# Moving the generation of the state-space matrices from the mixer into the FFN ahead of it, on GpSimd

## The reference, cut to what matters

```
for l in range(2):                                    # two layers, 512 latent and 256 context tokens, width 1024
    x, xc = x + 0.5 * gate * rms(swiglu(pre(x))), ...         # FFN 1 (1024 -> 2 x 2816 -> 1024)
    h = pre(x) @ w_in[l]                              # 512 SSM channels and 512 Fourier channels
    lam_bar = exp(lam * dt);  b_bar = ((lam_bar - 1) / lam) * b      # weights alone
    y_ssm = glu(d_skip * u + sum over both directions of Re(C @ scan(lam_bar, b_bar @ u)))
    y_f   = real(fft2(h_fourier)) @ w_fmix[l]
    x = x + gate * rms(concat(y_ssm, y_f) @ w_out[l])
    x = x + 0.5 * gate * rms(swiglu(pre(x)))                  # FFN 2
```

## Time and profile before

| | |
|---|---|
| median of 3 runs | 3126.36 us (3124.43 to 3127.66) |
| the profiled execution | 3122.22 us, with a span of 3120.4 us |
| mean granted TensorE clock | 0.924 of 2.4 GHz |
| TensorE matmul busy | 2833.4 us (91%) |
| VectorE busy | 1733.7 us (56%) |
| ScalarE busy | 696.0 us (22%) |
| GpSimd busy | 390.3 us (13%) |
| DMA | 313.84 MB, mean 101 GB/s |

### The profile page before, as it was taken

The page is one execution under the profiler, slowest core; times in us unless marked ns, Lnnn a source line. Parts: engine busy times, 40 slices in busy tenths (PEclk is TensorE's granted clock), DMA queues, the critical chain, the costliest instruction groups (busy, mean ns, idle before and its releaser), DMA issues.

```text
span 3120.4 us, 41582 instructions
## 1 busy us (share of the span) xinstructions
PE 2833.4 (91%) x16334; PEld 2627.6 (84%) x16334; DVE 1733.7 (56%) x2513; ACT 696.0 (22%) x921; POOL 390.3 (13%) x609
## 2 busy tenths in 40 slices
PE   6999999977987879999999799999977877899997
PEld 4999999966856869999999799999966656688886
DVE  5766666576354386666665633333367545544444
ACT  4211111132202231111112311111133102322222
POOL 1000000027702100000001000000027622100001
PEclk9999999986796989999999899999987686899998
DMA  7443333213353224343431122221222463223331
GB/s 254 135 126 117 121 121 121 81 34 125 126 187 95 61 68 126 111 127 114 128 114 56 39 64 64 60 67 54 70 44 95 149 194 84 66 88 94 101 94 47
DMA packets 343593, 313.84 MB, mean 101 GB/s; under 512 B 52544, under 2 KB 318664, under 8 KB 338888
## 3 DMA queue, kind: packets, MB, share of 16 engines
q1 hardware_dynamic: 280136, 204.59, 22.1%
q10 hardware_dynamic: 59264, 89.07, 8.7%
q0 software_dynamic: 4096, 18.88, 1.7%
HBM read 280.58 MB, written 31.92 MB: 100 GB/s over the span
## 4 chain that ended last, share of the span: by engine, by line
PE 78%; DVE 9%; POOL 6%; DMA 2%; ACT 2%; issue 2%; SPq 0%; ACTq 0%; DVEq 0%; POOLq 0%
PE ps L434 69%; PE ps L1131 2%; PE ps L560 2%; PE ps L807 1%; PE ps L1177 1%; DVE tmpN L885 1%; DMA E_d<-EG 1%; DVE rmsX L894 1%; DVE xT L773 1%; DVE hL L903 1%; DVE tmpN L911 1%; ACT wH L419 1%; POOL raw L1078 1%; DVE zb L1530 1%; DVE zd L1531 1%
## 5 line engine op out<-in xcount | busy, mean ns | idle before, releaser
L434 PE MATMUL ps<-hH,wH 128*128 128x384 f32 (+1 forms) x2880 | 1004.1, 349 | 66.9 <-DVE hL L903 46.3
L434 PE MATMUL ps<-hL,wH 128*128 128x384 f32 (+1 forms) x2880 | 997.3, 346 | 0.0
L434 PE MATMUL ps<-hH,wL 128*128 128x384 f32 (+1 forms) x2880 | 996.5, 346 | 0.0
L426 DVE TENSOR_TENSOR wL<-raw,wH 128x1024 fp32r<-128x1024 f32 x300 | 366.5, 1234 | 522.2 <-ACT wH L419 520.8
L434 PEld LDWEIGHTS ps<-hH,wH 128*128 128x128 f32 x2880 | 549.1, 191 | 90.6 <-issue 49.4
L434 PEld LDWEIGHTS ps<-hL,wH 128*128 128x128 f32 x2880 | 549.1, 191 | 18.0
L434 PEld LDWEIGHTS ps<-hH,wL 128*128 128x128 f32 x2880 | 548.2, 190 | 18.2
L419 ACT ACTIVATE wH<-raw 128x1024 fp32r<-128x1024 f32 x300 | 310.7, 1050 | 580.5 <-PE ps L434 576.4
L434 PE MATMUL ps<-midH,wH 128*128 128x384 f32 (+1 forms) x1232 | 423.8, 344 | 9.8 <-DVE wL L426 9.8
L434 PE MATMUL ps<-midH,wL 128*128 128x384 f32 (+1 forms) x1232 | 423.2, 343 | 0.0
L434 PE MATMUL ps<-midL,wH 128*128 128x384 f32 (+1 forms) x1232 | 423.1, 343 | 0.0
(11 more groups left out here) (252 smaller groups left out, 2436.9 us busy)
## 6 DMA issues: line engine op xcount, KB each, us to landing
raw<-in_ffn_gu_dram SPq DMA_DIRECT2D x176, 512.0 KB, 3.9
adaW<-in_w_ada_dram ACTq DMA_DIRECT2D x40, 1536.0 KB, 7.0
raw<-in_ffn_down_dram SPq DMA_DIRECT2D x88, 512.0 KB, 3.7
raw<-in_w_in_dram SPq DMA_DIRECT2D x16, 512.0 KB, 4.3
VT_d<-VTm ACTq DMA_DIRECT2D x8, 1024.0 KB, 3.9
W_d<-W ACTq DMA_DIRECT2D x8, 1024.0 KB, 5.0
raw<-in_w_out_dram SPq DMA_DIRECT2D x16, 512.0 KB, 4.4
VTs<-VT_d SPq DMA_DIRECT2D x8, 1024.0 KB, 5.4
```

Source lines behind the costliest of these rows:

```text
L426: nc.vector.tensor_tensor(wL[:, n % SPLIT_SLOTS, :], raw[:, n % RAW_SLOTS, :], wH[:, n % SPLIT_SLOTS, :].bitcast(f32), ALU.subtract).then_ ...
L434: ins = nc.tensor.matmul(dst, a, b, start=first and n == 0, stop=last and n == 3 * len(pairs) - 1)
```

## The change

1. The whole generation leaves the mixer. It becomes `gen_*` and runs in F1_0 (for M0) and F1_1 (for M1), cut into 8 pieces (quarter and direction) of half the size. V, W, b_bar, the pivots and the phases are made by GpSimd (`gen_pool`); TensorE's transposes of a piece stand inside a step's down product after m=3, its lags behind the down product; ScalarE copies out of PSUM.
2. Room: the tables take the place of `xT` in SBUF during the FFN. GpSimd stores `xT` to scratch `x_d` first (3 MB), and loads it back after the last piece; the norm after the FFN waits for it. PSUM's banks 6 and 7 go to the generation, so these two FFNs have three slots in place of four. `raw` has three slots everywhere.
3. The lags now use stationary tiles of 64 x 32 (`Bw`, half zeros) that go to four column groups of the array in turn, where they were 64 x 16 tiles in one column group.
4. D is added to the strip's centre by GpSimd (`skip_lag`), so `skip` and its reload of u are gone.
5. The loops over FFN steps are unrolled. SyncE's order in the mixer is new: the tables of quarter 0 are loaded before the projections end.
6. The small loads: `crow` takes 2 DMAs for a layer, not 32, and TensorE reorders it with 32 products against the identity.

```diff
-RAW_SLOTS, SPLIT_SLOTS = 4, 3
+RAW_SLOTS, SPLIT_SLOTS = 3, 3
+PIECES = 2 * HC
...
+        F.gen = Section("gen", GEN_COUNTS) if gen else None
+        F.slots = 3 if gen else 4
...
     def ffn_tensor(pe, F, pre):
...
+        for s in range(NPH - 1):
+            for i in range(4):
+                ride = F.ride0 + 2 * s + i // 2 if F.ride0 is not None and i % 2 == 0 else None
+                gate_up(4 + 6 * s + i, 4 + 12 * s + i, ride)
+            piece = s - 1 if F.gen and 1 <= s <= PIECES else None
+            down(8 + 6 * s, 8 + 12 * s, s, None if piece is None else lambda: gen_turn(pe, F.gen, piece))
+            if F.gen and s == 0:
+                gen_columns(pe, F.gen)
+            if piece is not None:
+                gen_lags(pe, F.gen, piece)
...
+        def lag_term(c0, c1, a, dd, rhs, first, last):
+            for p in range(QP):
+                for g2 in range(2):
+                    half = slice(g2 * NST, (g2 + 1) * NST)
+                    ins = nc.tensor.matmul(ps[32 * p:32 * p + 32, 6 + g2, c0:c1], Bw[half, a, dd, p, :], rhs(half, a, dd, p),
+                                           start=first, stop=last)
...
+    def gen_pool(pool, F):
...
+        pool.wait_ge(h_lo, KC * F.pre.nth + KC)
+        pool.dma_start(x_d, xT[:].rearrange("p k t -> p (k t)")).then_inc(x_spill, 16)
+        pool.wait_ge(x_spill, S.n0["x_spill"] + 16)
...
+        def state_in(i):
...
+            if i:
+                pool.wait_ge(vt_ps, S.n0["vt_ps"] + i)
+                pool.wait_ge(vt_store, S.n0["vt_store"] + 16 * i)
...
+        for i in range(PIECES):
+            state_in(i)
+            if i and i % 2 == 0:
+                skip_lag(i // 2 - 1)
+            state_out(i)
+            if i == 0:
+                pivots()
+            phases(i)
+        skip_lag(HC - 1)
...
+        pool.dma_start(xT[:].rearrange("p k t -> p (k t)"), x_d).then_inc(x_back, 16)
...
     def mix_tensor(pe, M, pre):
...
-        for q in range(HC):
-            if q:
-                proj(2 * q)
-                proj(2 * q + 1)
-            matrices(q)
-
+        for m in range(2, 8):
+            proj(m)
...
         for q in range(1, HC):
             turn(q)
-            if q >= 2:
-                skip(q - 2)
             turn_back(q, 0, zb, zd, ALU.subtract, True)
-        skip(HC - 2)
```

More of the change, by code:

```diff
@@ L325, in __init__, with make_ffn @@
             made[kind] += 1
-    def make_ffn(tag, layer, gu, down, tok0, ride0):
+    def make_ffn(tag, layer, gu, down, tok0, ride0, gen):
         nonlocal unit
@@ new lines, in tile_slot, with wait_tile @@
+    def tile_slot(F, g):
+        return g % F.slots
+    def wait_tile(pe, F, g):
+        if g < 4:
+            pair, part = 0, g
+        elif (g - 4) % 12 < 4 and g < 4 + 12 * (NPH - 1):
+            pair, part = (g - 4) // 12 + 1, (g - 4) % 12
+        else:
+            done = 12 * (NPH - 1) if g >= 4 + 12 * (NPH - 1) else 12 * ((g - 4) // 12) + 4
+            p, m = min((g - 4) // 12, NPH - 1), g - 4 - done
+            pe.wait_ge(down_read, F.n0["down_read"] + KC * (p + 1) + m + 1)
+            return
+        if part % 2 == 0:
+            pe.wait_ge(gate_read, F.n0["gate_read"] + 2 * pair + part // 2 + 1)
+        else:
+            pe.wait_ge(up_read, F.n0["up_read"] + 2 * pair + part // 2 + 1)
@@ new lines, in ffn_tensor, with gate_up, down @@
+    def ffn_tensor(pe, F, pre):
+        def gate_up(i, g, ride):
+            if g >= F.slots:
+                wait_tile(pe, F, g - F.slots)
+            if ride is not None:
+                ada_columns(pe, ride, 2 * tile_slot(F, g), TOK // 2)
+            n = F.base + i
+            pe.wait_ge(w_lo, n + 1)
+            wh, wl = wtile(n)
+            project(F.tok0, tile_slot(F, g), [(wh[:, k, :], wl[:, k, :]) for k in range(KC)], hH, hL).then_inc(w_used, 1)
+        def down(i, g, p, between=None):
+            n = F.base + i
+            pe.wait_ge(w_lo, n + 2)
+            pe.wait_ge(mid_lo, F.n0["mid_lo"] + 2 * p + 2)
@@ L664, in ffn_scalar @@
         for j in range(2):
[L665 to L676 removed]
+            gate(2 * j, 2 * j, j, None)
@@ new lines, in ffn_scalar @@
+            up(2 * j + 1, j)
+        for s in range(NPH - 1):
+            for j in range(2):
+                i, f = 4 + 6 * s + 2 * j, 2 + 2 * s + j
+                gate(i, 4 + 12 * s + 2 * j, f, None if F.ride0 is None else F.ride0 + 2 * s + j)
+                up(i + 1, f)
+            piece = s - 1 if F.gen and 1 <= s <= PIECES else None
+            if piece is not None:
+                gen_take_turned(act, F.layer, F.gen, piece)
+            split_hi(act, F.base + 8 + 6 * s + 3)
+            split_hi(act, F.base + 9 + 6 * s + 3)
+            if F.gen and s == 0:
+                gen_take_columns(act, F.gen)
+            if piece is not None:
+                gen_take_lags(act, F.gen, piece)
@@ L733, in ffn_vector @@
-        loop(dve, F, body, 0 if F.ride0 is None else 1)
-        down(4 + 12 * BODIES, 0, NPH - 1)
+            up(2 * j + 1, 2 * j + 1, j)
+        for s in range(NPH - 1):
+            more = F.ride0 is not None and s < NPH - 2
+            if F.ride0 is not None:
+                ada_steps(dve, F.ride0 + 2 * s + 1, 0, STEPS)
+            for j in range(2):
+                i, g, f = 4 + 6 * s + 2 * j, 4 + 12 * s + 2 * j, 2 + 2 * s + j
+                if j and more:
+                    ada_steps(dve, F.ride0 + 2 * s + 2, 0, KC)
+                split_lo(dve, F.base + i + 3)
+                up(i + 1, g + 1, f)
+            down(8 + 6 * s, 8 + 12 * s, s, F.ride0 + 2 * s + 2 if more else None)
@@ L1004, in mix_sync @@
         sp.wait_ge(y_ps, M.n0["y_ps"] + HC)
-        for i in range(12, 18):
-            load_unit(sp, i, 0, M.base, units[i])
+        load_units(12, 18)
     STATE_SEGS = ((0, 0, NCH - 1, slice(1, NCH)), (1, 0, CCH - 1, slice(CCH - 2, None, -1)),
@@ L1585, in rest_g @@
             tt(gL[:, m, 0:T], G[:, m, 0:T], gH[:, m, 0:T].bitcast(f32), ALU.subtract).then_inc(g_lo, 1)
-        for m in range(HC - 1):
+        for m in range(HC):
             rest_g(m)
-        skip(HC - 1)
-        rest_g(HC - 1)
         def times_gate(m):
```

703 lines of the change are left out of this document (331 added, 372 removed).

## The result

| | median of 4 runs | range |
|---|---|---|
| before | 3126.98 us | 3124.43 to 3127.66 |
| after | 2991.86 us | 2989.59 to 2992.80 |

The ratio is 0.9568, with a 95% interval from 0.9552 to 0.9585: 135 us faster, where 87 had been forecast. One execution of a later variant (e1_spill_early) took 6359.7 us for a reason that no trace shows, and no reading uses it. The profiled execution of the changed kernel has a span of 2987.4 us, 133.0 less than before.

The account below looks back on a forecast made before the run. TensorE was taken to bound F1_0 and F1_1, while engines waited on each other in the mixers' generation. 3122 - 201 of gains + 114 of costs = 3035 us, 3039 as median; range 2980 to 3115 us.

Parts of the forecast that it names:

- rival 2: Both FFNs: additions are cheap, tiles overlap by more than two, GpSimd hardly holds VectorE; 59 us added, 2984 us; chance 0.19.
- Mixers: M0 and M1: the generation's stretch shrinks to the projections left, gaining 93.5 us and 103.7 us.
- `skip`: Both mixers: removing these VectorE instructions gains 4 us, with nothing to 6 possible.
- TensorE's added work: F1_0 and F1_1: transposes 7.2, columns 2, lags 16, waits and shape changes 5, together 30 us in each FFN.
- overlap by two: Lags in F1_0 and F1_1: tiles overlap by about two, as L1194's do, so 2.0 us a piece, 16 for eight.
- overlap by eight: Lags in F1_0 and F1_1: if tiles ran eight at a time, TensorE's additions would be 20 us in each FFN.
- GpSimd against VectorE: F1_0: GpSimd's instructions hold VectorE's ada steps and splits, so TensorE waits: 41 us, from nothing to 87; F1_1 2 us.
- Three slots: F1_0 and F1_1: one PSUM slot fewer makes a down product's fourth tile wait, 5 us and 1 us.
- The spill: Start of F1_0: storing xT (3 MB) alongside the first two ada loads costs 5 us, between 0 and 12.
- Reload and raw slots: The reload of xT hides behind the FFN's last step, and three raw slots cost nothing.
- rival 4: F1_0 and F1_1: the clock falls behind each piece, 57 us for each FFN, 3153 us; chance 0.09.
- Rival 3: F1_0: VectorE becomes the bound, 69 us a step against TensorE's 57, costing 96 us; 3089 us; chance 0.16.

Follow-up runs that it names:

- e1_spill_early: The changed kernel, but GpSimd starts the spill of xT when the first chunk of the FFN's input is ready, not the eighth: median 2982.2 us.
- e4: The changed kernel, but lags go through all terms of one 64 x 32 tile before the next tile: median 3025.1 us.
- e2: The changed kernel, but in F1_0 GpSimd's 12 products and sums of each piece work on 64 of 512 columns: median 2971.5 us, F1_0 16.4 shorter.
- e3: The changed kernel, but each of GpSimd's 8 products of a piece is made twice, in both FFNs: median 3027.5 us, F1_0 37.5 longer.

## Why the prediction was right, and where not

The sign was right, and so were the gain in the mixers and the kinds of cost that the sum names. The range (2980 to 3115) held the time, but only as it reached down to rival 2: the number lay 47 us too high, outside the forecast's own 3005 to 3070 and 8 us from rival 2's 2984. Two terms were mis-sized, the overlap of the lags and what a hold costs.

- **Mixers**, 93.5 and 103.7 us: 92.7 and 101.3. The Fourier weights stood 51.4 and 41.0 us behind projection 1 (51 and 39 forecast); M1 lost 2 us in two waits for ScalarE, 0.58 and 0.69 us, and the slower products behind them. There was no wait for UC, VTs or the DFT.
- **`skip`**, 4 us: the two mixers' later parts are 9.9 us shorter. 5.5 of it stand between the Fourier weights and the states, which now run nearer to the full level (a gain that the forecast had cancelled against SyncE's loads); 4.4 are left for `skip`.
- **TensorE's added work**, 30 us for each FFN: 17.9 in F1_1, that is 2.0 for the columns (2.02 in the chain) and 2.0 a piece for transposes (0.87), lags and changes of shape. The step that failed is the overlap by two, taken from L1194. The lags took 0.55 and 1.13 us in turn, 0.8 in the mean where 2.0 was taken; that is 9 of the 12 us. The serial price was right as far as a run shows it (e4's slow pieces took 4.49 us where 4.6 was reckoned), and the wide ones overlap by 32 x 0.095 / 0.4 = 8 (the first to the last start, 0.4 us). Of the Trainium skill's rules in "TensorEngine Tiling (Array Packing)", Key Properties, that of the independent tiles gave 4 us a layer, an estimate. About 7 were measured, as the short ones overlap less (64 records in 0.6 us, serially 1.6). The waits and changes of shape, put at 5 us, took under 2. A slip besides: with overlap by eight the sum gives 18 us and not 20.
- **GpSimd against VectorE**, 41 us: e2 gives 16 for the wide instructions. The mechanism holds: ada rows alternate, splits are held, L720 is not. The step that failed is the number of holds times their price. I counted ten ada rows in a ride and added a whole instruction of GpSimd, 1.3 us, for each. In the four steps with a wait seven rows were held, at 0.9 us each, and the two splits lost 1.3 us together: 12.5 + 7 x 0.9 + 1.3 = 20.1 us, where I had 26. Measured from the end of the down product, TensorE could start the columns after 19.5 to 20.4 us. It came at 18.9 us (20.2 forecast, since the lags are shorter), so it waited 0.6 to 1.5 us and not 6. In the steps between, six rows were held and it did not wait. In step 0 twelve were held and it waited 6.1 us (8 forecast). The mean of 1.0 us for the ada rows was 0.81. The Trainium skill, "SBUF — State Buffer", Who interferes with whom, says that whichever of the two engines starts first keeps the shared port pair for its whole instruction. The trace agrees on which rows are held, but not in full on the price: one after the other a free ada row and a free product would take 0.54 + 1.18 = 1.72 us from start to start, and 1.44 were measured. It also says that a row with one input contends if it runs in a mode that takes two ports, and `tensor_scalar` can. The trace agrees in that L522, with one input, went from 0.42 us to 1.44 beside a product; the mode itself is in no row.
- **Three slots**, 5 and 1 us: 2.7 us of waits and none. **The spill**, 5 us: 8 us of wait, worth 6.1 in F1_0 when taken away. The 3 MB of the spill and the 3 MB of ada loads went together, which puts VectorE's first row off from 88.61 to 98.98 us. **Reload and raw slots**, 0: the norm behind F1_0 took 37.0 us as before, and F2_0's 3.3 us more are for the most part two stretches at a lower clock (96 products in 18.34 and 18.50 us, 16.77 and 16.96 before).
- **The clock.** What rival 4 expected did not come: F1_1 ran at 1.00 from 1790 to 2255 us, through all eight pieces. But behind VectorE's waits F1_0 lost some 11 us, a term that the sum did not have.
- **Rivals.** Rival 2 described both failed steps (59 us in the FFNs; 68 measured). Against it I had set that GpSimd starts just as the ada steps do. That is true, and e3 shows what it costs once the slack is gone. Rival 3's bound was not reached: VectorE was busy for 465 of 643 us.

Together: 81 - 50 = 31 us in F1_0, 33 - 18 = 15 in F1_1 and 3 in the mixers make 49 of gain that the forecast lacked. The other FFNs and the norms took 3 of it back.

## What to carry to other kernels

When two engines lock each other out, read the price of a hold from a stretch in which they alternate: the distance from one row's start to the next, less the same distance where the row is free. Here it was 0.9 us, and the other engine's instruction is 1.1 us long. Then count how many rows are held ahead of a deadline, since only these matter. Compute how late that stretch may end, and put the other engine's long instructions elsewhere: here the same instructions in another order were worth 8 us in F1_0. Behind each short wait look for a stretch at the lower clock, which can cost as much as the wait. Move a large spill to where the DMA engines are idle, not to where the next loads start.

## What was not expected of the hardware

- Lags on eight tiles of 64 x 32: 16 instructions of 112 columns start within 0.4 us whether they go round the tiles or through them one by one, but with 16-column ones between them they run one after the other (4.5 us in place of 1.1).
- A VectorE row of 384 columns that alternates with GpSimd's 512-column products costs 1.44 us in place of 0.54, which is less than the two take one after the other (1.72).
- Waits of TensorE of 1.0 to 1.5 us were followed by stretches at a mean clock of 0.74 and 0.86 in some steps and by none in others, so that the same first FFN differed by 3 us from run to run.
- A third PSUM slot in place of a fourth cost 3.9 us where tiles have 384 columns and 12.5 where they have 256.
